# A fused two-block transformer kernel: the forget gate's row sums spread by four transfers in place of four matrix products, and another split of the memory's input chunks

## The chip, the cores and the metric

The kernel runs on one core of one Trainium2 chip. The metric is the time of one execution on the device in microseconds (us); a figure for a kernel is the median over several executions. The core has TensorE (PE, matrix products; PEld is its weight load), VectorE (DVE), ScalarE (ACT), GpSimd (POOL) and SyncE (SP), each with a queue of instructions that it works off in order. They wait for one another through semaphores. DMA engines, sixteen of them, move data; transfers are issued from the queues of SP, ACT and POOL.

## The reference, cut to what matters

Two transformer blocks are computed over 512 tokens of width 1024. The change lies in the first block's mixer, in which one of four parts is a "forgetting attention", and at its border to the cross attention to a memory of 256 tokens that follows.

```python
def forgetting_mixer(p, b_f):
    q, k, v = ...                                   # 4 heads of 64
    logf = jax.nn.log_sigmoid(p[..., 3 * G:] + b_f) # forget gate, one number per token and head
    c = jnp.cumsum(logf, axis=1).transpose(0, 2, 1) # row sums c[head, token]
    return from_heads(forgetting_attention(q, k, v, c))

# in forgetting_attention, per block of 128 queries
    s = einsum(q * scale, k) + ci[..., None] - c[:, :, None, :]
    s = where(kpos <= t, s, NEG_INF); o = softmax(s) @ v

def memory_cross_attention(xn, memn, w_q, w_kv, w_o):
    k, v = split(memn @ w_kv, 2)                    # memn = rms_norm(mem, g_mem)
    ...
```

The softmax cancels a term that is the same for all keys of a query, so the kernel adds to the scores only a term per key. That term is a row c[head, :] of 512 numbers, and since queries lie on the 128 partitions, the row must stand in every partition.

## The kernel before, in words

Matrices are multiplied in float32 by three products of split halves: the operands are rounded to a high part (ACT) and a remainder (DVE), and `product` (lines 475 to 477) multiplies high by high, low by high and high by low. All weights come as a stream of 315 units of 128 x 1024 numbers (512 KB). SP loads them into two buffers `w_raw` (a new load is issued when DVE has split the unit that was in the buffer), ACT writes `w_hi` (line 1126, in `split`), DVE writes `w_lo` (line 1693, in `split`), and PE uses them. A split of a unit waits until PE has finished the unit two before it.

The mixer. The input projections end with four units for the values (lines 612 to 634). Then PE starts on the output projection with the four mixer chunks that are ready: `early_unit(0)` makes two of its eight columns, 24 products. The loop over the 32 attention items t follows (lines 756 to 772). There a PE item holds: `turn(t - 3)` (transposes of probabilities, line 694, waits for DVE's probabilities), on even items `scores(t)` (line 685, waits for the softmax minimum of the items before), in items 0 to 3 `gate_rows(t)`, in items 0 to 2 `early_unit(t + 1)`, from item 4 on `memory_half(t - 4)` (half a unit of the memory's key and value projection), and from item 5 on `weigh`. Items 0 to 7 and 16 to 23 are the dilated attention with a bias table, items 8 to 15 and 24 to 31 the forgetting attention.

The forget gate. DVE makes the cumulative sums, four rows `c_rows` on partitions 0 to 3 (line 1856). PE turns them by line 640 into columns, which ACT copies to `nci` (line 1244). To bring each row to all partitions, `gate_rows(h)` on PE multiplies a 4 x 128 table of zeros and ones (`heads`, loaded by POOL) by the four rows (line 663), in float32 without a split; the trace has two records for each such product. ACT's `gate_rows(h)` copies the result from PSUM into `proj[:, 1 + h, :]` (line 1252). POOL waits for all of these (line 2543) and then adds the `nci` column and the causal mask, two instructions per item of the forgetting attention (lines 2551 and 2555), always two items ahead. DVE's `least(t)` (line 1928) adds that bias to the scores and takes the minimum; for item 8 it is the first that reads a POOL bias.

The memory. ACT issues three transfers for the memory's input (lines 1258 to 1261, 1 MB together) right after line 1244. `memory_in(c)` for the chunks c = 0 to 7 runs on ACT (lines 1309 and 1312: the high part and the square) and on DVE (line 1957: the low part), and POOL adds the squares up (line 2541). Items 0, 1, 2 and 3 take two chunks each, on ACT and DVE ahead of the split of the item's weight unit. `memory_half(0)` on PE in item 4 waits for the low part of all eight chunks and for the four gate rows. Directly behind it PE makes the sums of squares (line 753).

On DVE, the order inside an item is: low part of turned probabilities (`lo`, line 1944), `probs` (lines 1935 and 1937), `least` (1928), staging of the next heads (1903 and 1904), `memory_in` (1957), the split (1693), and the sums of the two early columns (`early_sum`, line 1756), which wait for PE. Ahead of the loop stand the staging of the first heads and the sums of columns 0 and 1.

Ahead of the loop ACT stages the first heads (line 1271); the first scores on PE (line 685) wait until DVE has made the remainders of that staging (lines 1904 and 1903).

Of the kernel before, what the change touches and what calls it, by code (L numbers as in the profile page):

```python
# [32 lines left out]
ACT = mybir.ActivationFunctionType  # L33
AX = mybir.AxisListType

P = 128
D = 1024
S = 512
KC = D // P
# [8 lines left out]
N_FORGET = G // HD  # L48
# [16 lines left out]
XQ_FIRST = 3  # L65
XO_EARLY = (10, 10, 11, 11, 12, 12, 13, 13, 14, 15, 16, 17, 18, 19, 20, 20)
MEM_LAG = 4
DIFF_SLOTS = 4
BAND = S + S - P
LAST = 4  # L70
# [52 lines left out]
def bass_two_blocks(nc, weights, x_cols, mem_cols, positions, params, consts, dil_table, head_rows, alibi_table, head_picks,  # L123
# [6 lines left out]
    def stage(name, *signals):  # L130
        return {s: sem(f"{name}_{s}") for s in signals}
# [18 lines left out]
    with ctx:  # L150
# [29 lines left out]
        mix = dict(hi=sb("mix_hi", [P, KC, S], F32R, s_ctx), lo=sb("mix_lo", [P, KC, S], F32R, s_ctx))  # L180
# [155 lines left out]


        loads = stage("loaded", "input", "second", "rest", "con", "early", "tables", "later")
        N_EARLY, N_TABLES, N_MEM, N_SPATIAL_TABLES = 2, 3, 3, 2
        w_loaded = [sem("weights_loaded_0"), sem("weights_loaded_1")]  # L340
        idle = sem("idle_zeroed_done")
        first_half = sem("first_half_hi_lo")
# [12 lines left out]
        rows_rms_ready = sem("row_rms_ready")  # L355
        rows_ready = sem("r_rows_ready")
        w_in = stage("w_in", "evacuated", "v_ready")
        gate = stage("gate", "steps", "abs_exp", "c", "turned", "rows")
        rot = stage("rope", "steps", "trig", "swapped", "prod", "prod_cos", "done")
        small = stage("mixer", "steps", "conv", "pooled", "product", "hi")  # L360
        mix_ready = sem("mix_ready")
# [110 lines left out]
        def _(pe):  # L472
# [181 lines left out]
            early_unit(0)  # L654
            pe.wait_ge(w_in["v_ready"], TB)

            def gate_rows(h):

                if h == 2:
                    pe.wait_ge(gate["rows"], 1)  # L660
                if h >= 2:
                    pe.wait_ge(gate["rows"], h)
                nc.tensor.matmul(ps[:, 6 + h % 2, :], rope["heads"][0:N_FORGET, h * P:(h + 1) * P],
                                 mix["c_rows"][0:N_FORGET, :], start=True, stop=True).then_inc(gate["turned"], 1)

            def group_buffers(t, names):
                return (at1[f"{name}{t // 8 % 2}"] for name in names)  # L670
# [44 lines left out]
            def memory_half(t):  # L715
# [8 lines left out]
                if half == 0:  # L724
                    pe.wait_ge(w_ready, u + 1)
                    if m == 0:
                        pe.wait_ge(mem["lo"], KC)
                        pe.wait_ge(gate["rows"], 1 + N_FORGET)
                    if 2 <= m < KC:
                        pe.wait_ge(mem["k_ready"], m - 1)  # L730
                if m == KC:
# [25 lines left out]
            for t in range(MIX_ITEMS + 5):  # L757
                if 0 <= t - 3 < MIX_ITEMS:
                    turn(t - 3)
                if t < MIX_ITEMS and t % 2 == 0:  # L760
                    scores(t)
                if t < N_FORGET:
                    gate_rows(t)
                if t < LAST - 1:
                    early_unit(t + 1)
                if 0 <= t - MEM_LAG < 4 * KC:
                    memory_half(t - MEM_LAG)
                if t >= 5 and (t - 5) % 8 >= 2:
                    if t % 8 == 7:
                        weigh(t - 7)  # L770
                        weigh(t - 6)
                    weigh(t - 5)
# [345 lines left out]
        def _(act):  # L1118
# [125 lines left out]
            nc.scalar.activation(mix["nci"][:].rearrange("p b h -> p (b h)"), ps[:, 2, 0:TB * N_FORGET], ACT.Copy,  # L1244
                                 scale=-1.0).then_inc(gate["rows"], 1)

            def gate_rows(h):

                if h == 0:
                    act.wait_ge(mix_ready, 4)  # L1250
                act.wait_ge(gate["turned"], h + 2)
                nc.scalar.activation(mix["proj"][:, 1 + h, :], ps[:, 6 + h % 2, :], ACT.Copy).then_inc(gate["rows"], 1)


            act.wait_ge(summed, KC)
            act.wait_ge(r_ready, 1)
            act.wait_ge(gate["c"], 1)
# [5 lines left out]

            act.wait_ge(rot["done"], 4)
            act.wait_ge(w_in["evacuated"], 17)
            act.wait_ge(w_in["v_ready"], TB)
            act.wait_ge(used, FIRST["w_in"] + 2 * KC + 5)

# [70 lines left out]
            for t in range(MIX_ITEMS + 6):  # L1339
                if 0 <= t - 4 < MIX_ITEMS:  # L1340
                    hi(t - 4)
                if 0 <= t - 1 < MIX_ITEMS:
                    exp(t - 1)
                if t % 8 == 5 and t > 8:
                    output(t // 8 - 1)
                g = t // 8 + 1
                if t % 8 == 1 and g < 2 * GC:
                    stage_qk(g)
                if t % 8 == 6 and g < 2 * GC:
                    stage_v(g)  # L1350
                if t < N_FORGET:
                    gate_rows(t)
                if t < KC // 2:
                    memory_in(2 * t)
                    memory_in(2 * t + 1)
                if t < LAST:
                    split(FIRST["w_out_early"] + 2 + t)
                memory_out(t - MEM_LAG)

# [327 lines left out]
        def _(dve):  # L1687
# [295 lines left out]
            for t in range(MIX_ITEMS + 6):  # L1983
# [10 lines left out]
                    stage_qk(g)  # L1994
                if t % 8 == 6 and g < 2 * GC:
                    stage_v(g)
                if t < KC // 2:
                    memory_in(2 * t)
                    memory_in(2 * t + 1)
                if t < LAST:  # L2000
                    split(FIRST["w_out_early"] + 2 + t)
                if t < LAST - 1:
# [466 lines left out]
        def _(pool):  # L2469
# [13 lines left out]
            pool.dma_start(rope["pos"][:], positions).then_inc(loads["early"], 16)  # L2483
            pool.dma_start(lam_in[:], lambdas).then_inc(loads["early"], 16)
            pool.dma_start(rope["pool_w"][:], pool_blocks).then_inc(loads["tables"], 16)
            pool.dma_start(rope["heads"][:], head_rows).then_inc(loads["tables"], 16)
            pool.dma_start(mix["dil"][:], dil_table).then_inc(loads["tables"], 16)
            sum_squares("mix")

# [50 lines left out]
                    pool.wait_ge(mem["summed"], c)  # L2540
                    nc.gpsimd.tensor_tensor(memory["acc"][:], memory["acc"][:], memory["sq"][:, c % 2, :], ALU.add).then_inc(mem["summed"], 1)

            pool.wait_ge(gate["rows"], 1 + N_FORGET)
            with pool.Fori(0, GC) as c:
                for m in range(8):
                    b, h = m // 2, m % 2
# [212 lines left out]
```

## Time and profile before

| | before |
|---|---|
| time, median of 3 runs | 1888.62 us (1888.59 to 1890.22) |
| the profiled execution's own time | 1889.28 us |
| its span, first to last instruction | 1887.4 us |
| busy: PE, DVE, ACT, POOL | 1863.0, 1098.3, 768.0, 261.1 us |
| granted TensorE clock, mean | 0.992 of full speed |
| bytes moved | 174.48 MB, 92 GB/s over the span |

The profile comes from one execution with the hardware profiler on. Its time is 0.66 us above the median of the runs; 1.9 us of it lie outside the span. Times in rows are microseconds from the start of the span. A busy PE is not a PE at its peak: consecutive products overlap, so what a product costs is read from the start of one to the start of the next.

### The profile page before, as it was taken

Reading aid. Unit: us, or ns where it says so; the run is one execution under the profiler, and the core shown is the slowest. Engines: PE = TensorE matmul, PEld = TensorE weight load, DVE = VectorE, ACT = ScalarE, POOL = GpSimd, SP = SyncE. Lnnn points to the kernel's source line nnn. Section 1 sums busy time; section 2 is a strip of 40 time slices with the busy share of each in tenths; the row PEclk is TensorE's granted clock in tenths of the full one; section 3 lists DMA queues with packets and bytes.
Section 4 is the critical chain, followed back from the end, with each engine's and each line's share of the span. In section 5 each row is a group of like instructions: output and inputs, shape, how many; then the busy total and the mean of one; then the engine's idle time right before and its main releaser. Section 6 shows DMA issues by size and latency. Waiting matters only on the chain.

```text
span 1887.4 us, 24931 instructions
## 1 busy us (share of the span) xinstructions
PE 1863.0 (99%) x8782; PEld 1526.1 (81%) x8782; DVE 1098.3 (58%) x1577; ACT 768.0 (41%) x1182; POOL 261.1 (14%) x206
## 2 busy tenths in 40 slices
PE   9999999999999999999999999999999999999998
PEld 7877888788888888888888888888787888888886
DVE  6867976676777524677544442254888654444223
ACT  4226654355545413563333222144557433323212
POOL 4803320020000001301100000021643110000001
PEclk9999999999999999999999999999998999999998
DMA  5232322122222332222222322332211222222232
GB/s 181 92 109 73 103 97 76 56 90 100 90 99 89 123 100 89 93 87 90 98 97 95 98 95 96 100 104 96 68 56 34 68 95 96 98 97 95 97 100 78
DMA packets 62837, 174.48 MB, mean 92 GB/s; under 512 B 5428, under 2 KB 23988, under 8 KB 62648
## 3 DMA queue, kind: packets, MB, share of 16 engines
q1 hardware_dynamic: 61424, 169.50, 26.8%
q10 hardware_dynamic: 1016, 2.92, 0.5%
q0 software_dynamic: 336, 1.25, 0.2%
q8 instruction: 39, 0.64, 0.1%
q14 instruction: 22, 0.18, 0.0%
HBM read 171.54 MB, written 2.10 MB: 92 GB/s over the span
## 4 chain that ended last, share of the span: by engine, by line
PE 91%; DVE 6%; ACT 1%; issue 1%; DMA 0%; POOL 0%; SPq 0%; POOLq 0%; DVEq 0%; ACTq 0%
PE ps L475 29%; PE ps L477 29%; PE ps L476 29%; DVE w_lo L1693 1%; PE ps L1017 1%; PE ps L1028 1%; DMA x<-in_x_cols 0%; PE ps L972 0%; DVE at_e L1928 0%; DVE sg_z L2225 0%; ACT w_hi L1126 0%; PE ps L503 0%; DVE sg_t L2221 0%; PE ps L685 0%; DVE sg_u L2230 0%
## 5 line engine op out<-in xcount | busy, mean ns | idle before, releaser
L1693 DVE TENSOR_TENSOR w_lo<-w_raw,w_hi 128x1024 fp32r<-128x1024 f32 x314 | 405.5, 1291 | 456.4 <-ACT w_hi L1126 455.9
L475 PE MATMUL ps<-xg_hi,w_hi 128*128 128x512 f32 (+1 forms) x1448 | 564.7, 390 | 4.2 <-DVE w_lo L1765 1.9
L476 PE MATMUL ps<-xg_lo,w_hi 128*128 128x512 f32 (+1 forms) x1448 | 557.6, 385 | 0.0
L477 PE MATMUL ps<-xg_hi,w_lo 128*128 128x512 f32 (+1 forms) x1448 | 557.3, 385 | 0.0
L1126 ACT ACTIVATE w_hi<-w_raw 128x1024 fp32r<-128x1024 f32 x314 | 330.5, 1052 | 533.7 <-PE ps L477 529.7
L475 PEld LDWEIGHTS ps<-xg_hi,w_hi 128*128 128x128 f32 x1448 | 272.3, 188 | 70.9 <-DVE w_lo L1693 7.8
L477 PEld LDWEIGHTS ps<-xg_hi,w_lo 128*128 128x128 f32 x1448 | 272.4, 188 | 54.7
L476 PEld LDWEIGHTS ps<-xg_lo,w_hi 128*128 128x128 f32 x1448 | 272.6, 188 | 53.3 <-issue 1.0
L475 PE MATMUL ps<-hid_hi,w_hi 128*128 (+1 forms) x528 | 205.5, 389 | 0.0
L477 PE MATMUL ps<-hid_hi,w_lo 128*128 (+1 forms) x528 | 205.4, 389 | 0.0
L476 PE MATMUL ps<-hid_lo,w_hi 128*128 (+1 forms) x528 | 205.4, 389 | 0.0
L2476 POOL COPY square_sum<-squares 128x512 f32<-128x512 f32 x7 | 4.8, 686 | 947.0 <-ACT squares L1141 946.0
L475 PEld LDWEIGHTS ps<-hid_hi,w_hi 128*128 128x128 f32 x528 | 99.1, 188 | 20.9 <-DVE w_lo L1693 0.4
L476 PEld LDWEIGHTS ps<-hid_lo,w_hi 128*128 128x128 f32 x528 | 99.1, 188 | 20.7
L477 PEld LDWEIGHTS ps<-hid_hi,w_lo 128*128 128x128 f32 x528 | 99.1, 188 | 20.4
L2479 POOL TENSOR_TENSOR square_sum<-square_sum,squares 128x512 f32<-128x512 f32 x49 | 78.3, 1597 | 61.3 <-ACT squares L1141 60.3
L475 PE MATMUL ps<-w_hi,xg_hi 128*128 128x512 f32 x192 | 77.4, 403 | 0.3 <-DVE w_lo L1693 0.3
L1714 DVE TENSOR_TENSOR conv_a<-ps,r_cols 128x512 f32<-128x512 f32 x44 | 30.4, 691 | 78.5 <-PE ps L477 78.5
L477 PE MATMUL ps<-w_hi,xg_lo 128*128 128x512 f32 x192 | 74.8, 390 | 0.0
L476 PE MATMUL ps<-w_lo,xg_hi 128*128 128x512 f32 x192 | 74.8, 390 | 0.0
L1543 ACT ACTIVATE gate<-conv_g 128x512 f32<-128x512 f32 x44 | 27.8, 632 | 109.0 <-DVE conv_g L1714 109.0
L1699 DVE SCALAR_TENSOR_TENSOR xg_lo<-x,par,xg_hi 128x512 fp32r<-128x512 f32 x56 | 60.7, 1098 | 6.7 <-ACT xg_hi L1191 6.6
(375 smaller groups left out, 2460.6 us busy)
## 6 DMA issues: line engine op xcount, KB each, us to landing
w_raw<-in_weights SPq DMA_DIRECT2D x315, 512.0 KB, 3.3
out_cols<-result SPq DMA_DIRECT2D x8, 256.0 KB, 2.2
x<-in_x_cols SPq DMA_DIRECT2D x2, 512.0 KB, 5.7
x<-in_x_cols SPq DMA_DIRECT2D x1, 1024.0 KB, 8.9
squares<-in_mem_cols ACTq DMA_DIRECT2D x1, 512.0 KB
sp_w<-in_spatial ACTq DMA_DIRECT2D x1, 512.0 KB
sp_b<-in_spatial_bias ACTq DMA_DIRECT2D x1, 512.0 KB
dil<-in_dil_table POOLq DMA_DIRECT2D x1, 448.0 KB, 4.8
```

Of the source, the lines that this page charges most:

```text
L475: nc.tensor.matmul(to, wh, xh, start=start, stop=False)
L476: nc.tensor.matmul(to, wh, xl, start=False, stop=False)
L477: return nc.tensor.matmul(to, wl, xh, start=False, stop=stop)
L1017: mm = nc.tensor.matmul(ps[:, h, 0:w], q_[rows, block_], k_[rows, 0:w], start=k == 0, stop=k == 2)
L1028: mm = nc.tensor.transpose(ps[:, 4 + n % 2, j * P:(j + 1) * P], at3["e"][:, 2 * (n % DIFF_SLOTS), j * P:(j + 1) * P], ident)
L1126: nc.scalar.activation(w_hi[:, u % 2, :], w_raw[:, u % 2, :], ACT.Copy).then_inc(w_hi_ready, 1)
L1543: nc.scalar.activation(ffn["gate"][:], ffn["tg"][:], ACT.Silu).then_inc(st["gated"], 1)
L1693: nc.vector.tensor_tensor(w_lo[:, u % 2, :], w_raw[:, u % 2, :], w_hi[:, u % 2, :].bitcast(F32), ALU.subtract).then_inc(w_ready, 1)
L1699: nc.vector.scalar_tensor_tensor(out=xg_lo[:, c, :], in0=x[:, c, :], scalar=column(gain, c), in1=xg_hi[:, c, :].bitcast(F32), op0=ALU.mult ...
L1714: return nc.vector.tensor_tensor(to, ps[:, bank, 0:cols], r_cols[:] if r is None else r, ALU.mult).then_inc(signal, 1)
L2476: nc.gpsimd.tensor_copy(sums[:], squares[:, 0, :]).then_inc(summed, 1)
L2479: nc.gpsimd.tensor_tensor(sums[:], sums[:], squares[:, c % 2, :], ALU.add).then_inc(summed, 1)
```

## The change

The four products by the table, their copies out of PSUM and the table's load are gone. ACT issues four transfers in their place, each of which reads one row of `c_rows` (one partition, 2 KB) and writes it to all 128 partitions (256 KB). They are issued after the memory's three transfers, ahead of the first staging, on the same queue; POOL waits for them. The memory's chunks are split 2, 3, 3 over the items 0 to 2 on ACT and DVE.

```diff
+MEMORY_IN = {0: (0, 1), 1: (2, 3, 4), 2: (5, 6, 7)}
...
-        N_EARLY, N_TABLES, N_MEM, N_SPATIAL_TABLES = 2, 3, 3, 2
+        N_EARLY, N_TABLES, N_MEM, N_SPATIAL_TABLES = 2, 2, 3, 2
...
 @@ TensorE
-            def gate_rows(h):
-
-                if h == 2:
-                    pe.wait_ge(gate["rows"], 1)
-                if h >= 2:
-                    pe.wait_ge(gate["rows"], h)
-                nc.tensor.matmul(ps[:, 6 + h % 2, :], rope["heads"][0:N_FORGET, h * P:(h + 1) * P],
-                                 mix["c_rows"][0:N_FORGET, :], start=True, stop=True).then_inc(gate["turned"], 1)
...
                     if m == 0:
                         pe.wait_ge(mem["lo"], KC)
-                        pe.wait_ge(gate["rows"], 1 + N_FORGET)
...
-                if t < N_FORGET:
-                    gate_rows(t)
                 if t < LAST - 1:
                     early_unit(t + 1)
 @@ ScalarE
-            def gate_rows(h):
-
-                if h == 0:
-                    act.wait_ge(mix_ready, 4)
-                act.wait_ge(gate["turned"], h + 2)
-                nc.scalar.activation(mix["proj"][:, 1 + h, :], ps[:, 6 + h % 2, :], ACT.Copy).then_inc(gate["rows"], 1)
...
             act.wait_ge(rot["done"], 4)
             act.wait_ge(w_in["evacuated"], 17)
+            act.wait_ge(mix_ready, 4)
+            for h in range(N_FORGET):
+                act.dma_start(mix["proj"][:, 1 + h, :], mix["c_rows"][h:h + 1, :].unsqueeze(1).to_broadcast([1, P, S])
+                              ).then_inc(gate["spread"], 16)
             act.wait_ge(w_in["v_ready"], TB)
...
-                if t < N_FORGET:
-                    gate_rows(t)
-                if t < KC // 2:
-                    memory_in(2 * t)
-                    memory_in(2 * t + 1)
+                for c in MEMORY_IN.get(t, ()):
+                    memory_in(c)
 @@ VectorE
-                if t < KC // 2:
-                    memory_in(2 * t)
-                    memory_in(2 * t + 1)
+                for c in MEMORY_IN.get(t, ()):
+                    memory_in(c)
 @@ GpSimd
-            pool.dma_start(rope["heads"][:], head_rows).then_inc(loads["tables"], 16)
...
-            pool.wait_ge(gate["rows"], 1 + N_FORGET)
+            pool.wait_ge(gate["rows"], 1)
+            pool.wait_ge(gate["spread"], 16 * N_FORGET)
```

## Rows read from the trace of the kernel before

**Rows 1.** The page's part 1: busy time of the engines, share of the span, instructions.

```profile
PE 1863.0 (99%) x8782; PEld 1526.1 (81%) x8782; DVE 1098.3 (58%) x1577; ACT 768.0 (41%) x1182; POOL 261.1 (14%) x206
```

**Rows 2.** PE's timeline around the gate's products: start, duration, engine, line, operation; [idle before].

```profile
140.12 0.33 PE L685 MATMUL ps<-at_khi,at_qhi 64*128 64x128 f32 x2
...
140.60 1.12 PE L663 MATMUL ps<-c_rows,heads 4*128 4x512 f32 x2
141.65 0.50 PE L475 MATMUL ps<-mix_hi,w_hi 128*128 128x512 f32 x1
...
146.79 0.39 PE L476 MATMUL ps<-mix_lo,w_hi 128*128 128x512 f32 x1
147.01 0.39 PE L477 MATMUL ps<-mix_hi,w_lo 128*128 128x512 f32 x1
...
148.72 0.40 PE L476 MATMUL ps<-mix_lo,w_hi 128*128 128x512 f32 x1
...
161.43 1.12 PE L663 MATMUL ps<-c_rows,heads 4*128 4x512 f32 x2
162.56 0.33 PE L694 MATMUL ps<-con,at_e 128*128 128x128 f32 x1
...
165.07 0.36 PE L475 MATMUL ps<-xg_hi,w_hi 128*128 128x256 f32 x1 [1.37 <-issue]
...
167.88 0.44 PE L694 MATMUL ps<-con,at_e 128*128 128x128 f32 x2 [0.81 <-DVE at_e L1937]
```

**Rows 3.** DVE's timeline: first staging, memory chunks, early sum, probabilities, item 8's bias.

```profile
137.94 0.68 DVE L1903 TENSOR_TENSOR at_klo<-proj,at_khi 128x512 fp32r<-128x512 f32 x1
...
157.48 0.67 DVE L1957 SCALAR_TENSOR_TENSOR xg_lo<-square_sum,par,xg_hi 128x256 fp32r<-128x256 f32 x1 [0.22 <-ACT xg_hi L1309]
...
161.42 0.69 DVE L1756 TENSOR_TENSOR x<-ps,x 128x512 f32<-128x512 f32 x1 [0.86 <-PE ps L477]
...
162.22 0.29 DVE L1937 TENSOR_SCALAR at_e<-at_e,at_inv 128x128 f32<-128x128 f32 x1
...
164.31 0.65 DVE L1957 SCALAR_TENSOR_TENSOR xg_lo<-proj,par,xg_hi 128x256 fp32r<-128x256 f32 x1 [0.22 <-ACT xg_hi L1309]
...
178.35 0.28 DVE L1928 CUSTOM_DVE_ANT_0 at_e<-ps,proj 128x128 f32<-128x128 f32 x1
```

**Rows 4.** ACT's timeline: the last memory transfer's issue, staging, a chunk, two splits.

```profile
135.47 0.45 ACTq L1261 DMA_DIRECT2D proj<-in_mem_cols  x1
136.46 0.63 ACT L1271 ACTIVATE at_qhi<-proj 128x512 fp32r<-128x512 f32 x1 [1.71 <-DVE mix_v L1891]
...
142.31 0.50 ACT L1309 ACTIVATE xg_hi<-squares,par 128x256 fp32r<-128x256 f32 x1
...
157.66 1.05 ACT L1126 ACTIVATE w_hi<-w_raw 128x1024 fp32r<-128x1024 f32 x1
...
173.60 1.05 ACT L1126 ACTIVATE w_hi<-w_raw 128x1024 fp32r<-128x1024 f32 x1
```

**Rows 5.** Busy time by engine in a stretch: PE, PEld, DVE, ACT, POOL; clock; DMA share; GB/s.

```profile
180.00:200.00 20.00, 19.06 (x181) 17.22 (x180) 19.71 (x48) 12.23 (x28) 9.82 (x11) 1.00 0.26 85
```

**Rows 6.** POOL's timeline: the mask added to the first bias, item 8's.

```profile
166.00 1.32 POOL L2555 TENSOR_TENSOR proj<-proj,con 128x128 f32<-128x128 f32 x1
```

**Rows 7.** DMA issues: what, queue, count, size, median us from issue to landing.

```profile
w_raw<-in_weights SPq DMA_DIRECT2D x315, 512.0 KB, 3.3
...
x<-in_x_cols SPq DMA_DIRECT2D x1, 1024.0 KB, 8.9
...
heads<-in_head_rows POOLq DMA_DIRECT2D x1, 256.0 KB, 4.1
```

**Rows 8.** Stretches of 1 us behind the memory's transfers, columns as in rows 5.

```profile
140.00:141.00 1.00, 1.00 (x8) 0.70 (x8) 0.77 (x2) 0.00 (x0) 0.00 (x0) 1.00 0.81 276
141.00:142.00 1.00, 1.00 (x4) 0.30 (x3) 0.12 (x2) 0.18 (x1) 0.00 (x0) 1.00 0.18 48
```

**Rows 9.** SP's timeline: issue of the weight load that ACT's split at 157.66 reads.

```profile
146.06 0.34 SPq L417 DMA_DIRECT2D w_raw<-in_weights  x1
```

More of the change, by code:

```diff
@@ L357, in bass_two_blocks @@
         w_in = stage("w_in", "evacuated", "v_ready")
-        gate = stage("gate", "steps", "abs_exp", "c", "turned", "rows")
+        gate = stage("gate", "steps", "abs_exp", "c", "turned", "rows", "spread")
         rot = stage("rope", "steps", "trig", "swapped", "prod", "prod_cos", "done")
```

## The prediction

> **What bounds the kernel now.** I read the page's busy times first. PE is busy 99% of the span [rows 1], so time is won only where PE's own queue gets shorter or a wait in it goes. Everything outside the stretch from 135 to 180 us is untouched by the edit, so I then read PE's timeline there [rows 2]. It shows two things: products by the table that fill PE for about 1.1 us each, four times, and two waits just behind them, 1.37 and 0.81 us. The timelines of DVE and ACT [rows 3, 4] say who ends those waits. Last I looked at what follows: from 180 to 200 us DVE is busy 19.71 of 20 us and PE 19.06 [rows 5]. There both engines run without slack, each in order, so what is gained before 180 is kept only if DVE gets there earlier as well, and a DVE that is held at item 8 gives it back.
>
> **Part 1, the four products leave PE.** Item 0: from 140.60 to the next product at 141.65, 1.05 us. Item 1: from the product at 147.01 to the one at 148.72 there are 1.71 us; the normal step is 147.01 - 146.79 = 0.22, so two steps are 0.45 and the product with its switches costs 1.26. Item 2 has the pattern of item 0, 1.05. Item 3: 161.43 to 162.56, 1.13 [rows 2]. Sum 4.49.
>
> Not all of it counts. In item 3 the product stands ahead of turn(1) (162.56), which needs the probabilities of item 1. DVE makes them after the sum of the last early column, which waits for PE (161.42, 0.86 idle) and leads on to 162.22 + 0.29 = 162.51 [rows 3]. That path starts at PE's last early product and does not contain the gate's product, so without it PE waits there. I count item 3 at nothing: 4.49 - 1.13 = **3.36**, and turn(1) comes at 162.56 - 3.36 = 159.2.
>
> **Part 2, the memory's chunks.** memory_half(0) starts at 165.07 after 1.37 idle, released by the low part of chunk 7, which ends at 164.31 + 0.65 = 164.96 [rows 2, 3]. Those chunks stood in item 3, and on ACT behind the copy of the fourth product. Now they stand in item 2. There the second chunk's low part ended at 157.48 + 0.67 = 158.15 [rows 3]; everything is earlier by the two products of items 0 and 1 (1.05 + 1.26 = 2.31) and a third chunk is added. A chunk costs ACT a high part of 0.50 and a square that is not longer [rows 4], under 1.0 us, which covers DVE's 0.67. So the last low part is there by 158.15 - 2.31 + 1.0 = 156.8, while PE wants it at 165.07 - 1.37 - 3.36 = 160.3. The wait goes: **1.37**. What is late next is the split of the memory's first unit, ACT's at 157.66 [rows 4]. It moves with the same terms to 157.66 - 2.31 + 1.0 = 156.4, with DVE's behind it near 158.7, still ahead of 160.3.
>
> The 0.81 before turn(2) at 167.88 [rows 2] is DVE's probabilities of item 2, late because in item 3 ACT and DVE still had two chunks ahead of the split. They now have none, about 2 x 0.7 on either engine, more than the wait. It goes: **0.81**.
>
> **Part 3, what the new transfers cost their queue.** ACT issues four transfers at about 0.45 each, as at 135.47 [rows 4]: 1.8 us, from 135.92 to 137.72. The first staging at 136.46 [rows 4] moves by 1.26. The first scores on PE at 140.12 need DVE's remainder, 137.94 + 0.68 = 138.62 [rows 2, 3], now 139.88. Cover left: 0.24. From below the cost is nothing; from above, should an issue with a repeated row take a third longer (0.6), the staging is 0.6 later still and PE waits 0.4. I take nothing, by the row at 135.47. Behind the staging, ACT in item 0 would wait for the memory's input anyway.
>
> ACT also loses four copies and its waits for PE, all hidden. POOL's issue of the table (one transfer of 256 KB [rows 7]) lay beside work, and POOL's next instruction waited for ACT: nothing. DVE's wait for the tables was met long before: nothing.
>
> **Part 4, when the rows arrive.** This is the unknown term. The trace has no transfer out of one partition. What waits for them is POOL, and behind POOL item 8's bias, read by DVE at 178.35 [rows 3], now near 178.35 - 5.5 = 172.8. POOL needs two instructions first; the mask's took 1.32 [rows 6], and I allow 2 us for both. So the rows have until **170.8**. The memory's transfers stand ahead of them in ACT's queue, and the DMA engines have worked those and a weight load off by about 141.2 [rows 8]. From below, a transfer of 256 KB costs what the memory's and the weights' bytes cost there, 276 GB/s [rows 8]: 1 us each, or, one landing after another, 4.1 each like the table [rows 7], which ends at 157.6. From above I take the slowest landing in the trace, 8.9 [rows 7], though that moved 1 MB among the first loads: four in a row are 35.6 us and end at 176.8, 6.0 late. The nearest row by size and shape is the table's, and I take it: nothing.
>
> **Sum.** 3.36 + 1.37 + 0.81 = 5.54, against the profiled execution's own 1889.28 us: 1883.7. The median of the runs is 0.66 lower than that execution, so the forecast for the median is 1888.62 - 5.5 = **1883.1**.
>
> The Trainium skill speaks against part 4. SBUF — State Buffer, section "Door 1: The DMA port swizzle", says that a DMA's rate depends on how many of 16 ports its partitions reach, and gives 27.6 GB/s for a tile on partitions 0 to 3. By that figure, an estimate, the megabyte read from these four partitions takes 38 us, ends near 179 and is 8 late, and the sum would be 5.5 less 8, a loss of 2 to 3. No row here shows such a transfer, so the trace neither agrees nor disagrees.
>
> **Rivals.** A, the forecast, 47%: 1881 to 1885.5.
>
> B, the rows come late for item 8, 25%. The sixteen DMA engines all read one partition at a time, and if that is slow the spread lasts until 176.8 or later instead of 170.8. DVE then stands at item 8, and with it the splits behind least(8) in its queue, as every microsecond past 170.8 is one of DVE's in a stretch where it has no slack [rows 5]. At the upper bound: 5.5 gained and 6.0 lost, so 1889.1. With a spread between 30 and 38 us the time lies from 1885.5 to 1891. For it: one source for all engines. Against it: nothing in the trace. (The skill's rule above is this mechanism.)
>
> C, slower: the spread stands in the way of the weights, 22%. The load issued at 146.06 is read by ACT at 157.66, 11.6 us later [rows 4, 9], and lands in 3.3 [rows 7]: a cover of 8.3. If a slow spread and a weight load take turns on each DMA engine, packet by packet, a load lasts as long as its share of the spread. A DMA engine has 8 rows of a load and 32 of the spread, so a load waits a quarter of the spread, 8.9, plus its own 3.3: 12.2. The first such load just misses its time; the next, queued behind it, is late by another 6 or so, and ACT and DVE stand in their splits with the attention queued behind. The split at 173.60 [rows 4] reads the third; it could not be ready before the spread ends at 176.8, and so comes 3.2 later than before, or some 4 with landing: 1892.6, and up to 1898 if the spread is slower than 8.9 a row. It decides from a spread of about 8 us a row; below that the cover of 8.3 holds. For it: weights and spread use the same DMA engines. Against: a fast spread ends before any of it matters.
>
> (The Trainium skill, DMA: Bandwidth & Descriptors, section "Queues, rings and completion order", has each DMA engine take turns between queues at packet granularity, which is C's premise; no row shows it yet.)
>
> D, the change saves only the products and not the waits, because ACT and DVE, not PE, set the pace of items 1 and 2 with three chunks in each, 6%: 3.4 less, 1885.3.
>
> **The numbers.** About 0.2%, 3.8 us, is what a measurement of this kernel can tell from no change. Faster by more than that is below 1884.8: nearly all of A, 0.44. Within it: the rest of A, D, nearly all of B and the mild end of C, 0.36. Slower, above 1892.4: most of C, a little of B, 0.20. The range takes in A, D, B and the lower half of C: 1880.8 to 1894. The likeliest case's own range is 1881 to 1885.5.
>
> **What would show it.** In the profile after: no product by the table; turn(1) near 159.2; memory_half(0) without a wait, near 160.3; turn(2) near 162.3; item 8's least near 172.8, with no idle time of DVE before it; the four transfers landing by 158. B shows as DVE idle before line 1928 in item 8, released by POOL, and POOL started by the transfers. C shows as ACT waiting at line 1126 for a transfer of weights between 150 and 180, and weight loads that take over 8 us to land. The forecast is wrong if a spread transfer takes more than about 7 us, or if the first scores start later than 140.12 by more than half a microsecond.

## The result and the profile after

| | before | after |
|---|---|---|
| time, median | 1888.72 us (1888.59 to 1890.22, 4 runs) | 1907.62 us (1907.07 to 1909.08, 4 runs) |
| ratio to before, 95% interval | | 1.0099 (1.0087 to 1.0111) |
| the profiled execution's own time, span | 1889.28, 1887.4 us | 1907.07, 1905.3 us |
| granted TensorE clock, mean | 0.992 | 0.986 |

The change costs 18.9 us, 1.0%. The forecast was 5.5 us faster, and the result lies above the top of its range.

The page of the kernel after, busy times, the two hardware DMA queues (packets, MB, share of 16 engines; q1 is SP's, q10 is ACT's) and the new transfers (size, median from issue to landing):

```profile
PE 1861.7 (98%) x8774; PEld 1527.7 (80%) x8774; DVE 1097.8 (58%) x1577; ACT 766.1 (40%) x1178; POOL 259.9 (14%) x205
...
q1 hardware_dynamic: 61424, 169.50, 27.1%
q10 hardware_dynamic: 1592, 3.97, 2.1%
...
proj<-c_rows ACTq DMA_DIRECT2D x4, 256.0 KB, 26.2
```

PE has less work than before (1861.7 us against 1863.0 in [rows 1]) and the span is 17.9 longer, so the loss is idle time or a slower clock. The last row is the first surprise: the median is 26.2 us from issue to landing, where the prediction took 4.1 for each.

The timeline of ACT after, which answers to [rows 4]: start, duration, operation; [idle before <- what ended it]. A row with "x4" runs from the first issue to the end of the fourth.

```profile
134.65 0.45 ACTq L1240 DMA_DIRECT2D proj<-in_mem_cols  x1
135.22 18.18 ACTq L1247 DMA_DIRECT2D proj<-c_rows  x4
153.50 0.63 ACT L1254 ACTIVATE at_qhi<-proj 128x512 fp32r<-128x512 f32 x1 [19.58 <-issue]
...
177.99 1.06 ACT L1113 ACTIVATE w_hi<-w_raw 128x1024 fp32r<-128x1024 f32 x1 [10.34 <-DMA w_raw<-in_weights]
```

ACT's timeline from 144 to 153 us, the fourth issue alone, and from the answer on the tile `c_rows` the spread of the four landings:

```profile
143.43 9.97 ACTq L1247 DMA_DIRECT2D proj<-c_rows  x1
```

```profile
DMA to landing us min/median/max: 12.4/26.2/33.6
```

Four issues take 18.18 us where the prediction had 1.8. The first costs 0.56; the last alone holds ACT's sequencer for 9.97. The first staging, at 136.46 in [rows 4], starts at 153.50. The shortest is the first transfer's, the longest the last's: the first lands at 135.2 + 12.4 = 147.6, the last at 143.4 + 33.6 = 177.0, so one row of 256 KB takes (177.0 - 147.6) / 3 = 9.8 us, or 27 GB/s.

The timeline of PE after, which answers to [rows 2]: the first scores, the next early products, turn(1) and turn(2).

```profile
155.71 0.48 PE L675 MATMUL ps<-at_khi,at_qhi 64*128 64x128 f32 x2 [16.34 <-DVE at_klo L1883]
...
157.56 0.63 PE L478 MATMUL ps<-mix_hi,w_lo 128*128 128x512 f32 x1
157.99 0.63 PE L476 MATMUL ps<-mix_hi,w_hi 128*128 128x512 f32 x1
...
176.19 0.27 PE L684 MATMUL ps<-con,at_e 128*128 128x128 f32 x1
182.12 0.48 PE L684 MATMUL ps<-con,at_e 128*128 128x128 f32 x1 [5.66 <-DVE at_e L1917]
```

There are two holes, 16.34 and 5.66 us. Behind the first, a product of the same shape starts every 0.43 us (157.56 to 157.99), where it is 0.22 in [rows 2].

Stretches of the kernel after: busy time of PE, PEld, DVE, ACT, POOL; granted clock; DMA share; GB/s. They answer to [rows 8].

```profile
136.00:138.00 2.00, 2.00 (x10) 1.66 (x9) 0.60 (x1) 0.00 (x0) 0.00 (x0) 1.00 0.90 310
...
140.00:154.00 14.00, 0.00 (x0) 0.00 (x0) 0.00 (x0) 0.50 (x1) 0.00 (x0) 0.61 0.89 30
154.00:158.00 4.00, 2.29 (x10) 1.92 (x11) 3.73 (x9) 3.98 (x9) 1.22 (x2) 0.50 1.00 141
...
182.00:187.00 5.00, 4.88 (x22) 4.22 (x23) 3.27 (x12) 2.75 (x6) 0.00 (x0) 0.50 0.53 191
```

From 140 to 154 us the DMA engines are busy 0.89 of the time and move 30 GB/s; with the memory's input, from 136 to 138, as busy as that they move 310. In the same 14 us PE, DVE and POOL do nothing. The clock is 0.50 (the lower level, 1.2 GHz) behind each of the two holes of PE.

The chain of waits from 130 to 200 us of the kernel after names the two that hold the end: start, duration, what.

```profile
143.43 9.97 ACTq L1247
...
159.52 18.44 DMA w_raw<-in_weights
177.99 1.06 ACT w_hi L1113
```

**Where the 18.9 us are.** One version below, via_hbm, runs the same engine work with another transfer. From ACT's `nci` copy (134.58 before, 133.76 after, 134.74 in via_hbm) to item 8's first biased minimum (178.35, 196.09, 172.70) it is 43.77 us before, 62.33 after, 37.96 in via_hbm. After is 18.56 longer there. It entered the stretch 0.82 earlier, so item 8 comes 17.74 later, and the whole span is 17.9 longer: the loss is all in this stretch. The last row of [rows 3] stands in DVE's timeline after so:

```profile
196.09 0.28 DVE L1908 CUSTOM_DVE_ANT_0 at_e<-ps,proj 128x128 f32<-128x128 f32 x1
```

The stretches between these two moments, before, after and in via_hbm, columns as above:

```profile
134.58:178.35 43.77, 40.07 (x217) 30.17 (x218) 31.46 (x71) 26.72 (x60) 8.05 (x12) 1.00 0.29 95
```

```profile
133.76:196.09 62.33, 39.65 (x209) 32.58 (x210) 31.03 (x71) 25.01 (x56) 7.37 (x12) 0.81 0.69 82
```

```profile
134.74:172.70 37.96, 35.45 (x209) 28.98 (x210) 32.18 (x71) 25.01 (x56) 9.93 (x12) 1.00 0.41 136
```

After and via_hbm have the same 209 PE records. After is 24.37 longer: 39.65 - 35.45 = 4.20 is the same work, part of it at half clock, and (62.33 - 39.65) - (37.96 - 35.45) = 20.17 is idle time. So the change gained 43.77 - 37.96 = 5.81 as intended, and the slow spread took 24.4.

### The profile page after: what moved, and what is told of

The parts are those of the page before. It is cut to its first block, busy times and chain, and to the rows that moved or that the text cites. A ratio compares the mean times of both kernels' runs of the same rounds, so it can differ in the third digit from the quotient of the medians.

```text
span 1905.3 us, 24913 instructions
## 1 busy us (share of the span) xinstructions
PE 1861.7 (98%) x8774; PEld 1527.7 (80%) x8774; DVE 1097.8 (58%) x1577; ACT 766.1 (40%) x1178; POOL 259.9 (14%) x205
## 4 chain that ended last, share of the span: by engine, by line
PE 89%; DVE 6%; DMA 1%; issue 1%; ACTq 1%; ACT 1%; POOL 0%; SPq 0%; POOLq 0%; DVEq 0%
PE ps L476 29%; PE ps L478 28%; PE ps L477 28%; DVE w_lo L1673 1%; PE ps L1004 1%; DMA w_raw<-in_weights 1%; ACTq L1247 1%; PE ps L1015 1%; PE ps L959 0%; DMA x<-in_x_cols 0%; DVE at_e L1908 0%; PE ps L675 0%; ACT w_hi L1113 0%; DVE sg_z L2204 0%; PE ps L504 0%
## 6 DMA issues: line engine op xcount, KB each, us to landing
proj<-c_rows ACTq DMA_DIRECT2D x4, 256.0 KB, 26.2
```

## The experiments

Two theories stood behind the first runs. The theory: the spread itself does it, with its slow reads of one partition. Its rival: it is a matter of where it stands in ACT's queue, and another order or queue would do. A third question is whether the gain forecast for PE was there at all. All edits are to the kernel after, except where it is said.

**no_spread.** Leaves out the gate's row sums (the bias has no such term).

```diff
-            for h in range(N_FORGET):
-                act.dma_start(mix["proj"][:, 1 + h, :], mix["c_rows"][h:h + 1, :].unsqueeze(1).to_broadcast([1, P, S])
-                              ).then_inc(gate["spread"], 16)
...
-            pool.wait_ge(gate["spread"], 16 * N_FORGET)
```

> The changed kernel without its four transfers and without POOL's wait for them; the forgetting attention then adds stale numbers in place of the row sums (left out). It prices parts 1 and 2 of the prediction alone. If the whole loss comes from the transfers, this runs 5.5 us faster than the kernel before, about 1883.2, with turn(1) near 159, memory_half(0) unwaited near 160 and turn(2) near 162. If taking the products out or the 2, 3, 3 split costs something by itself, it is at or above 1888.7.

Measured: 1884.25 us (1883.26 to 1886.62), ratio to before 0.997 (0.9958 to 0.9982); the kernel before was 1889.56 us beside this run and the next three. The whole loss hangs on the four transfers. In its trace PE has two waits up to turn(1), of 1.72 us for the sum of an early column and of 1.07 ahead of turn(1):

```profile
154.76 0.76 PE L476 MATMUL ps<-mix_hi,w_hi 128*128 128x512 f32 x1 [1.72 <-DVE x L1733]
...
163.28 0.33 PE L684 MATMUL ps<-con,at_e 128*128 128x128 f32 x1 [1.07 <-DVE at_e L1914]
```

The traced execution took 1886.62 us, the longest of the six, so its moments are no measure of the gain: turn(1) comes at 163.28, not near 159, and item 8 is 40.57 us behind `nci`. Behind the wait of 1.72 the granted clock falls for a while (0.72 from 156 to 160), as it does behind the holes of the kernel after.

**pool_issue.** The same four transfers, issued by POOL about 6 us earlier.

```diff
+            pool.wait_ge(gate["c"], 1)
+            pool.wait_ge(mix_ready, 4)
+            for h in range(N_FORGET):
+                pool.dma_start(mix["proj"][:, 1 + h, :], mix["c_rows"][h:h + 1, :].unsqueeze(1).to_broadcast([1, P, S])
+                              ).then_inc(gate["spread"], 16)
```

> The same four transfers, issued from POOL's queue after the same events, so that ACT is not held while it issues them. Theory one, the loss is ACT's held queue: then the first scores start at 140 again, and the time is at most 2 us above the kernel before, with only item 8's bias late: 1883 to 1891. Theory two, one source partition feeds all DMA engines at some 27 GB/s and the weight loads stand behind it: then ACT is free at 136.5, but waits for weights at its first splits in the loop, 15 us and more, and the time stays near 1900 to 1910.

Measured: 1916.53 us (1916.33 to 1917.11), 1.0142 (1.0127 to 1.0158), worse than after. POOL's and ACT's timelines and two stretches of this kernel:

```profile
128.95 2.20 POOL L2512 DMA_DIRECT2D proj<-c_rows  x4 [35.34 <-DVE mix_lo L1862]
```

```profile
134.85 3.70 ACTq L1239 DMA_DIRECT2D square_sum<-in_mem_cols  x1
138.58 14.32 ACTq L1240 DMA_DIRECT2D proj<-in_mem_cols  x1
153.10 0.63 ACT L1251 ACTIVATE at_qhi<-proj 128x512 fp32r<-128x512 f32 x1 [18.49 <-issue]
...
174.06 0.51 ACT L1289 ACTIVATE xg_hi<-squares,par 128x256 fp32r<-128x256 f32 x1 [19.29 <-DMA proj<-in_mem_cols]
```

```profile
130.00:134.00 4.00, 4.00 (x21) 3.14 (x21) 0.94 (x2) 0.52 (x1) 1.15 (x3) 1.00 1.11 34
134.00:138.00 4.00, 4.00 (x20) 3.35 (x20) 3.29 (x5) 0.61 (x2) 0.00 (x0) 1.00 0.99 29
```

POOL gives its four issues in 2.2 us and is not held. But ACT, which now issues only the memory's input, is held for 3.70 and 14.32 us. So an issue is not held because of what it moves: the slow spread holds it, from another queue. Busy DMA engines alone are not enough either: ACT's first issue, at 134.49, took 0.33 while they had been busy with the spread since 130. The memory's input lands late (19.29 us of waiting on ACT), and PE waits 15.3 and 14.1 us. The rival falls here.

**memory_only.** The kernel before with the memory's chunks split 2, 3, 3 and the four products kept.

```diff
-                if t < KC // 2:
-                    memory_in(2 * t)
-                    memory_in(2 * t + 1)
+                for c in MEMORY_IN.get(t, ()):
+                    memory_in(c)
```

> The kernel before, products and copies kept, with only the memory's chunks split 2, 3, 3 over items 0 to 2. By the prediction's part 2 it wins the two waits of 1.37 and 0.81 us at most: 1886.5 to 1888.7. If ACT or DVE set the pace of items 1 and 2 with three chunks, it is slower than the kernel before by up to 1.5 us.

Measured: 1887.67 us (1887.14 to 1889.46, 11 runs), 0.9992 (0.9983 to 1.0002): not told apart from no change. In its trace the 1.37 ahead of memory_half(0) is gone, and item 8 comes 42.57 us behind `nci`, 1.20 less than before. But the wait ahead of turn(2) stayed, 1.02 us:

```profile
166.49 0.44 PE L695 MATMUL ps<-con,at_e 128*128 128x128 f32 x2 [1.02 <-DVE at_e L1937]
```

**via_hbm.** The rows take another road. POOL stores the four rows (8 KB) in device memory as soon as they are there, long before, and ACT issues one load that repeats them into all partitions.

```diff
+    c_store = nc.dram_tensor("c_store", (N_FORGET, S), F32, kind="Internal").ap()
...
+            act.wait_ge(gate["stored"], 16)
+            act.dma_start(mix["proj"][:, 1:1 + N_FORGET, :], c_store.unsqueeze(0).to_broadcast([P, N_FORGET, S])
+                          ).then_inc(gate["spread"], 16)
...
+            pool.wait_ge(gate["c"], 1)
+            pool.dma_start(c_store, mix["c_rows"][0:N_FORGET, :]).then_inc(gate["stored"], 16)
```

> The rows go to all partitions by another route: POOL writes the four rows (8 KB) to HBM when they are made, near 112 us, and ACT issues one transfer of 1 MB from there to all partitions where the changed kernel issues four. If the source in one partition is what is slow, this lands within about 8 us, no issue is held, and the kernel is 4.5 to 6 us faster than before: 1882.7 to 1884.2. If a repeated source, a megabyte of traffic beside the memory's input or ACT's later staging is what hurts, it is slow as well, above 1892, with an issue or a landing of over 15 us.

Measured: 1884.22 us (1883.32 to 1885.13, 8 runs), 0.9972 (0.9961 to 0.9983). The same megabyte now lands in 8.1 us, beside the memory's input and a weight load. The page's row of the load, and two stretches:

```profile
proj<-c_store ACTq DMA_DIRECT2D x1, 1024.0 KB, 8.1
```

```profile
140.00:142.00 2.00, 2.00 (x13) 1.46 (x12) 0.90 (x3) 0.26 (x1) 0.00 (x0) 1.00 0.97 386
142.00:144.00 2.00, 2.00 (x10) 1.62 (x9) 0.97 (x2) 2.00 (x5) 1.06 (x2) 1.00 0.85 311
```

Its issue takes 0.34, and the staging starts at 136.69. The theory holds: the destination, the bytes, the queue and the place are the same, the source differs. Up to turn(1) its PE has two waits, one of 0.66 for an early column's sum and the one ahead of turn(1):

```profile
160.09 0.33 PE L686 MATMUL ps<-con,at_e 128*128 128x128 f32 x1 [1.07 <-DVE at_e L1919]
```

**What about the source is slow?** The next four ask this, each run once, beside a kernel before of 1888.98 us in that run.

**wide_source.** Four transfers of 256 KB from 128 partitions to the same 128 (the row sums are left out, old numbers are copied).

```diff
-                act.dma_start(mix["proj"][:, 1 + h, :], mix["c_rows"][h:h + 1, :].unsqueeze(1).to_broadcast([1, P, S])
+                act.dma_start(mix["proj"][:, 1 + h, :], mix["proj"][:, 9 + h, :])
```

> Four transfers of 256 KB from the same place in ACT's queue, but each reads a tile on all 128 partitions (four chunks of q and k in place of the rows, so the bias is wrong; the row sums are left out). Theory: the single source partition is what is slow. Then each lands within 6 us of its issue, no issue is held over 1 us, and the time is near that of the kernel without the transfers, 1883 to 1886. Rival: any megabyte copied within SBUF from this queue is slow, or four more transfers behind the memory's three fill the queue. Then landings of over 12 us, ACT held for 15 us and a time above 1900.

Measured: 1885.51 us. They land in 6.3 us each (median):

```profile
proj<-proj ACTq DMA_DIRECT2D x4, 256.0 KB, 6.3
```

So a megabyte copied within SBUF is not slow in itself. The four issues take 3.44, still more than 1.8 (one of them 1.57, against the expectation), and the staging starts at 138.78; PE waits 1.61 for it.

**one_row.** Only head 0's transfer (the other three rows are left out).

```diff
-            for h in range(N_FORGET):
+            for h in range(1):
...
-            pool.wait_ge(gate["spread"], 16 * N_FORGET)
+            pool.wait_ge(gate["spread"], 16)
```

> Only the first of the four transfers (the rows of heads 1 to 3 are left out). Theory: a row takes 9.5 to 10 us on a rate of 27 GB/s, and an issue is held only while earlier spreads are in flight. Then this one lands within 13 us, ACT stages at 137, the weight load issued at 136.6 lands about 10 us late but still ahead of its use near 148, and the time is 1883 to 1888. Rival: even one such transfer holds ACT; then the first scores are late by 5 us or more and the time is above 1890.

Measured: 1882.50 us. It lands in 11.4, and while it is in flight the core's traffic is as low as after's:

```profile
140.00:144.00 4.00, 4.00 (x20) 3.31 (x19) 3.66 (x7) 3.97 (x9) 1.14 (x2) 1.00 0.84 26
```

But its issue takes 0.56, ACT goes on to the staging at 136.11, and PE has no wait there. One row is as slow as each of four. It delays the weight load issued behind it (at 136.85), which lands after 11.4 us instead of 3.3, but that costs ACT a wait of 1.60 and PE none.

**pieces_same** and **pieces_apart.** The megabyte in 16 transfers of 64 KB, each from one partition to 32. The first takes its sources from partitions 0, 1, 2, 3 in turn (the edit shown), the second from 0, 4, 8, 12 (`4 * h:4 * h + 1`). Both copy other numbers than the row sums.

```diff
+            for g in range(4):
+                for h in range(N_FORGET):
+                    act.dma_start(mix["proj"][32 * g:32 * g + 32, 1 + h, :],
+                                  mix["proj"][1 * h:1 * h + 1, 9:10, :].to_broadcast([1, 32, S])
+                                  ).then_inc(gate["spread"], 16)
```

> The megabyte cut into 16 transfers, each from one partition to 32: for each quarter of the destination the sources 0, 1, 2, 3 in turn (rows of a q chunk; the row sums are left out). With the source's group of partitions as the limit nothing changes by the order: POOL is released at 175 to 180, 27 GB/s. If the limit is one partition alone, neighbours in turn can overlap and it is over before 165.

> The same 16 transfers with the sources on partitions 0, 4, 8 and 12. If what limits is the port that a group of four partitions shares, four ports now work at a time: up to four times the rate, POOL's release 15 to 25 us sooner than in the run with sources 0 to 3. If the limit is one partition, or the whole path within SBUF, the two runs agree within 3 us.

Measured: 1917.85 and 1897.52 us. The stretches of pieces_same, then of pieces_apart, and ACT's issues in each:

```profile
148.00:172.00 24.00, 0.00 (x0) 0.00 (x0) 1.41 (x3) 2.17 (x5) 0.00 (x0) 0.50 0.89 27
```

```profile
140.00:144.00 4.00, 0.00 (x0) 0.00 (x0) 0.00 (x0) 0.00 (x0) 0.00 (x0) 0.97 1.02 187
144.00:148.00 4.00, 0.00 (x0) 0.00 (x0) 0.00 (x0) 0.00 (x0) 0.00 (x0) 0.50 0.89 81
148.00:152.00 4.00, 0.73 (x6) 0.75 (x6) 2.17 (x4) 2.94 (x7) 0.48 (x1) 0.50 0.73 61
152.00:156.00 4.00, 4.00 (x11) 3.12 (x10) 3.06 (x7) 3.97 (x8) 0.73 (x1) 0.50 0.00 0
```

```profile
136.40 33.33 ACTq L1248 DMA_DIRECT2D proj<-proj  x16
```

```profile
135.62 13.35 ACTq L1248 DMA_DIRECT2D proj<-proj  x16
```

With sources in partitions 0 to 3 the rate is 27 GB/s for 24 us; four apart, the whole is over by 152 us. Same bytes, sizes, count, queue and destinations: only which partitions are read differs. Four sources next to one another are no faster than one, four sources apart are. From 144 to 148 pieces_apart moves 81 GB/s with only ACT's queue moving, three times 27. Neither is faster than the kernel before, as the 16 issues keep ACT for 33.33 and 13.35 us (the four of the kernel after: 18.18).

**The last four** ask which form of the fast road is best. The kernel before was 1889.23 us in them (22 runs).

**hbm_early.** via_hbm with the load issued by POOL, ahead of the memory's input.

```diff
+            pool.wait_ge(gate["stored"], 16)
+            pool.wait_ge(mix_ready, 4)
+            pool.dma_start(mix["proj"][:, 1:1 + N_FORGET, :], c_store.unsqueeze(0).to_broadcast([P, N_FORGET, S])
+                          ).then_inc(gate["spread"], 16)
```

> The route over HBM with the load of 1 MB issued by POOL at 128 to 130, once the buffers are free, in place of ACT's at 136. The memory's input then has ACT's queue to itself and ACT's 3.4 us wait for it at item 0 shrinks. If that wait sets the pace of items 0 and 1, 0.5 to 1 us faster than with ACT's load; if PE does, no difference over 0.5 us. A loss of 1 us or more would mean that the weight load issued near 130 is now late.

Measured: 1884.74 us (1883.97 to 1886.65), ratio 0.9977 (0.9967 to 0.9986). It lands in 4.6 us instead of 8.1, to no benefit: the interval overlaps via_hbm's.

**hbm_old_split.** via_hbm with the memory's chunks 2, 2, 2, 2, as before.

```diff
-MEMORY_IN = {0: (0, 1), 1: (2, 3, 4), 2: (5, 6, 7)}
+MEMORY_IN = {0: (0, 1), 1: (2, 3), 2: (4, 5), 3: (6, 7)}
```

> The route over HBM with the memory's chunks split 2, 2, 2, 2 as before. It tells what the split is worth once the products are gone: by the prediction the waits of 1.37 and 0.81 us come back, partly, since item 3 is shorter without its product: 1 to 2.5 us slower than with 2, 3, 3. If the split is worth nothing, the two agree within 0.5 us.

Measured: 1883.74 us (1883.41 to 1884.26), ratio 0.9970 (0.9959 to 0.9981), the lowest median of the kernels that compute everything, though not told apart from via_hbm. The expected 1 to 2.5 us of loss did not come. Item 8 comes 38.43 us behind `nci`, against 37.96.

**hbm_four.** via_hbm with four loads of 256 KB, each repeating one row from device memory.

```diff
+                act.dma_start(mix["proj"][:, 1 + h, :], c_store[h:h + 1, :].unsqueeze(1).to_broadcast([1, P, S])
```

> The route over HBM with four loads of 256 KB, each repeating one row of 2 KB for all partitions, which differs from the changed kernel's transfers in the source alone. Theory: the source in one SBUF partition is slow, a repeated row as such is not. Then each lands within 8 us, no issue is held over 1 us, and the time is within 1 us of the single load's, 1883 to 1885. If repeating a row of 2 KB is what is slow, it looks like the changed kernel: above 1900.

Measured: 1884.75 us (1884.02 to 1886.23, 10 runs), ratio 0.9976 (0.9967 to 0.9985). The shape of the four transfers is after's, only the source is device memory:

```profile
proj<-c_store ACTq DMA_DIRECT2D x4, 256.0 KB, 6.2
```

The four issues take 2.47. One row repeated 128 times is not slow in itself.

**after_staging.** The four slow transfers behind the staging of the first heads in ACT's queue.

```diff
             stage_qk(0)
             stage_v(0)
+            act.wait_ge(mix_ready, 4)
+            for h in range(N_FORGET):
+                act.dma_start(mix["proj"][:, 1 + h, :], mix["c_rows"][h:h + 1, :].unsqueeze(1).to_broadcast([1, P, S])
+                              ).then_inc(gate["spread"], 16)
```

> The changed kernel with its four transfers issued just behind ACT's first staging. It takes ACT's hold off the first scores: they start at 140. If the hold at the staging was the loss, the time falls to about 1890. If the transfers block weights and ACT wherever they stand, ACT is now held ahead of item 0's chunks and split instead, PE stops some 6 us later, and the time stays within 4 us of the changed kernel's 1907.6.

Measured: 1908.71 us (1906.92 to 1909.18), ratio 1.0099 (1.0084 to 1.0115), the same as after's. The first scores stand in time again, and the loss comes back one step later. ACT's timeline, then PE's:

```profile
138.41 16.68 ACTq L1320 DMA_DIRECT2D proj<-c_rows  x2
...
180.23 1.06 ACT L1113 ACTIVATE w_hi<-w_raw 128x1024 fp32r<-128x1024 f32 x1 [13.93 <-DMA w_raw<-in_weights]
```

```profile
159.52 0.79 PE L476 MATMUL ps<-mix_hi,w_hi 128*128 128x512 f32 x1 [12.55 <-DVE x L1736]
```

What stands behind the held issues on ACT is now item 0's chunks and split, PE stops for 12.55 at the early columns, and the weight load still does not come. So the hold costs as much here, and its place ahead of the first staging is not the cause.

## Why the prediction was wrong, step by step

**Part 4, the step that failed.** "The nearest row by size and shape is the table's, and I take it" put a transfer out of one partition at 4.1 us. Each took 9.8, above the 7 that the prediction named as a sign of being wrong, and four in a row 39 (from about 137.8 to 177.0). Size and shape were the wrong likeness. The table comes from device memory; what sets the time is which partitions are read (pieces_same against pieces_apart). The upper bound of 8.9 was itself short by 0.9 a row. POOL's wait for the rows ended at 177.57, 6.8 past the 170.8 that the prediction allowed.

The rule of the Trainium skill that the prediction set against this step (SBUF — State Buffer, section "Door 1: The DMA port swizzle") holds with its number: 27.6 GB/s for partitions 0 to 3 there, 27 measured. By the same section, partitions 0, 4, 8 and 12 reach four ports, and pieces_apart agrees: faster, 81 GB/s from 144 to 148. With that rate in place of the table's, the prediction's own sum was a loss of 2 to 3 us, not 18.9: this step alone does not explain the result.

**Part 3, the second step that failed, unseen by any rival.** The upper bound for ACT's issues was "a third longer (0.6)", with 0.4 of waiting on PE. The first two took 0.56 and 0.61, as bounded. The third and fourth took 6.95 and 9.97: ACT was held at an issue while the slow spread was in flight. PE's 16.34 us of idle time stand behind this hold, the largest part of the loss. pool_issue shows that it hits issues of other data, on another queue than the slow one; SP's single issues (0.34 to 0.37 in this stretch) and POOL's four weren't held. wide_source and hbm_four show milder forms of it (3.44 and 2.47 for four). The prediction counted an issue as a fixed price of 0.45; here the same instruction cost between 0.56 and 9.97. The other sign of being wrong came true here: the first scores started at 155.71 instead of 140.12.

**Rival C, right in kind, with a mechanism that the trace doesn't bear out.** C had the weights late, and its signs came: ACT waits at the split, and loads take over 8 us. The load issued at 136.62 landed after 22.2 us, at 158.8; that of 159.52 after 18.4, at 177.9. The first cost nothing, as ACT reads it at 164.08; the second cost ACT 10.34 and PE 5.66. C also named the point of decision, 8 us a row, correctly: it was passed. But by "take turns on each DMA engine, packet by packet" a load would have taken 12.2. The two queues of the kernel after, from 135 to 150 us and from 150 to 165 (packets, MB, share of 16 engines; q1 is the weights', q10 the spread's and, at first, the memory's):

```profile
q10 hardware_dynamic: 624, 1.39, 92.6%
q1 hardware_dynamic: 1, 0.00, 0.0%
```

```profile
q10 hardware_dynamic: 220, 0.41, 83.5%
q1 hardware_dynamic: 527, 0.52, 9.9%
```

For 13 us the load moved one packet, and then all of its 512 KB beside the spread, with more packets than the spread. So it was put off, and not slowed by sharing packet for packet. What the traces show is an order: a load landed shortly behind the last row that had been issued before it. Here that is 158.8 behind the second row's 157.3, and 177.9 behind the fourth's 177.0. In one_row it is 148.3 behind 146.9, in after_staging 160.4 behind 159.3 and 180.2 behind 179.2. Why it is so is not shown. The turns between queues at packet granularity that the Trainium skill states (DMA: Bandwidth & Descriptors, "Queues, rings and completion order") are neither confirmed nor refuted by these rows, which don't show whether the DMA engines had the load's work before 150.

C's range, 1892.6 to 1898, fails on ACT's hold and on the clock; 1907.6 lies outside every rival's.

**Rival B's wait is there, and cost nothing.** POOL's timeline of the kernel after:

```profile
177.57 0.40 POOL L2530 TENSOR_TENSOR proj<-proj,nci 128x128 f32 x1 [8.70 <-DMA proj<-c_rows]
```

POOL waited 8.70 us for the rows. By then PE and DVE were held up by the rest, and item 8 came at 196.09. B's lower end was also mis-added: by its own terms a spread of 30 us ends 0.4 late and gives 1883.5, not 1885.5.

**The clock**, which no part had. Behind PE's two holes the granted clock is 0.50, the lower of its two levels, for 4.4 us (155.7 to 160.1) and 5.4 us (182.1 to 187.5): 4.20 us more for the same 209 records.

**Parts 1 and 2 were right in their sum.** They said 5.54; via_hbm, which has these parts without the slow spread, reaches item 8 5.81 earlier, and its median is 0.28% lower, about 5.3 us. Item 3's product counts for nothing, as forecast: with it gone PE waits 1.07 at turn(1), in no_spread, via_hbm and hbm_old_split alike.

**That the sum came out is in part luck.** Up to turn(1) via_hbm gains 27.98 - 25.35 = 2.63 where the prediction had 3.36; the new wait of 0.66 for an early column's sum, D's mechanism in small, is most of what is missing. From turn(1) to item 8 it gains 15.79 - 12.61 = 3.18 where the prediction had 1.37 + 0.81 = 2.18: besides these two, waits of 0.33 (at 171.19 before) and part of one of 1.01 (at 176.82) went that it had not counted. The two errors nearly cancel.

**The cause given for the two waits was wrong too.** The 1.37 and 0.81 were put down to the new split of the memory's chunks. With the split alone (memory_only) the wait at turn(2) is 1.02, and the time is no different. With the products gone and the old split (hbm_old_split), PE's waits here are 0.37, 1.07, 0.18, 1.01 and 0.15, and the time is that of via_hbm. Up to item 8 the split alone brings 1.20, the products' removal alone 43.77 - 38.43 = 5.34, both 5.81. So they overlap, and the waits went with the products: the split adds 0.47 in the traces (one of each kernel) and nothing that the runs tell.

What stays open: why ACT's queue holds at the third transfer and not at the second, and why a weight load on SP's queue lands only behind the rows issued before it. The traces show the durations but not what is full. POOL's queue, which held at none of four, was tried only with these four.

## What to carry to other kernels

Before moving a product to the DMA engines, ask which partitions each transfer reads: a repeat of one partition's row ran at 27 GB/s here, and the weight loads and memory transfers issued behind it landed late. Store the few rows in device memory early and load them back with the repeat (8 KB out, 1 MB in, 4 to 8 us), or use the old product. And don't count an issue from a busy engine as free while a slow transfer is in flight: look at its duration in the trace.

## What the hardware showed unexpectedly

- Sixteen DMA engines at 0.89 busy and 30 GB/s: busy share of the DMA engines says nothing of what they move. Read both columns.
- A DMA issue on ACT's queue lasted from 0.33 us to 14.32, the long ones with a slow spread in flight. In the profile it stands as ACT idle "<-issue", not as a wait for a DMA.
- POOL's issue of the same transfers was not held (2.20 us for four).
- A weight load issued behind a slow row is not slowed down but put off: one packet by 150 us, then 527 in under 9 us, and landed 0.9 to 1.5 us behind that row in all five cases.
